# Laying the RWKV-7 chunk pairs on the partition halves by head parity in a one-core hybrid encoder layer

## The reference

```
def step(state, inp):
    r_t, w_t, k_t, v_t, kk_t, a_t = inp
    sa = jnp.einsum('bhvk,bhk->bhv', state, -kk_t)
    state = (state * w_t[:, :, None, :] + sa[..., None] * (kk_t * a_t)[:, :, None, :]
             + v_t[..., None] * k_t[:, :, None, :])
    return state, jnp.einsum('bhvk,bhk->bhv', state, r_t)
```

## Time and profile before

| | |
|---|---|
| median of 3 runs | 1093.29 us (1093.26 to 1096.49) |
| the profiled execution's own time | 1094.79 us |
| its span in the trace | 1092.7 us |
| TensorE busy | 1055.2 us, 97% of the span |
| VectorE, ScalarE, GpSimd busy | 608.6, 451.3, 30.9 us |
| chain that ended last | TensorE 80%, VectorE 9%, ScalarE 5% |

### The profile page before, as it was taken

One profiled execution on the slowest core, in us unless ns is written; L12 is line 12 of the kernel. 1 busy time (PEld: TensorE's weight loads), 2 busy tenths in 40 slices (PEclk: granted clock), 3 DMA queues, 4 the chain that ended last, 5 costly groups with the idle time before them and its releaser, 6 DMA issues.

```text
span 1092.7 us, 19121 instructions
## 1 busy us (share of the span) xinstructions
PE 1055.2 (97%) x8117; PEld 844.4 (77%) x8117; DVE 608.6 (56%) x858; ACT 451.3 (41%) x575; POOL 30.9 (3%) x50
## 2 busy tenths in 40 slices
PE   8999999999998999999999999999999999999997
PEld 5788667778876787787667778888888888878885
DVE  3499875356443469758656388663444533252446
ACT  5523643233323476755555464571222122222233
POOL 0100001000000000020000110000000000000000
PEclk9999999999999999999999999999999999999999
DMA  9977534211126331196311495304343423222201
GB/s 339 317 257 245 171 106 131 71 51 61 44 66 224 118 104 69 41 270 239 115 69 49 146 336 179 130 20 153 117 154 116 142 90 109 85 90 104 93 23 77
DMA packets 106780, 145.29 MB, mean 133 GB/s; under 512 B 3252, under 2 KB 86440, under 8 KB 106696
## 3 DMA queue, kind: packets, MB, share of 16 engines
q1 hardware_dynamic: 93544, 109.25, 30.2%
q0 software_dynamic: 5664, 21.19, 5.7%
q10 hardware_dynamic: 7488, 13.63, 3.3%
HBM read 128.33 MB, written 15.73 MB: 132 GB/s over the span
## 4 chain that ended last, share of the span: by engine, by line
PE 80%; DVE 9%; ACT 5%; DMA 2%; issue 2%; SPq 1%; ACTq 0%; POOL 0%; DVEq 0%
PE bank L2211 78%; DVE wlo L1466 2%; DVE Z L1466 1%; DVE q_lev L1466 1%; DMA qk<-early_out 1%; DMA raw<-in_w_in 1%; ACT whi L942 1%; SPq L814 1%; DVE near L1955 1%; ACT gate_row L957 1%; DVE mg L1466 1%; DVE ada_acc L1469 0%; DVE qk L1466 0%; PE bank L2792 0%; PE bank L2499 0%
## 5 line engine op out<-in xcount | busy, mean ns | idle before, releaser
L2211 PE MATMUL bank<-hhi,whi 128*128 128x512 f32 (+1 forms) x800 | 320.9, 401 | 4.3 <-ACT gate_row L957 2.6
L2211 PE MATMUL bank<-hhi,wlo 128*128 128x512 f32 (+1 forms) x800 | 310.0, 387 | 0.0
L2211 PE MATMUL bank<-hlo,whi 128*128 128x512 f32 (+1 forms) x800 | 309.7, 387 | 0.0
L1466 DVE TENSOR_TENSOR wlo<-raw,whi 128x2048 fp32r<-128x2048 f32 (+1 forms) x80 | 166.3, 2079 | 241.9 <-ACT whi L942 236.1
L942 ACT ACTIVATE whi<-raw 128x2048 fp32r<-128x2048 f32 (+1 forms) x76 | 135.5, 1783 | 227.6 <-PE bank L2211 178.1
L2211 PEld LDWEIGHTS bank<-hhi,whi 128*128 128x128 f32 x800 | 151.0, 189 | 46.4 <-issue 11.0
L2211 PEld LDWEIGHTS bank<-hhi,wlo 128*128 128x128 f32 x800 | 151.0, 189 | 31.5
L2211 PEld LDWEIGHTS bank<-hlo,whi 128*128 128x128 f32 x800 | 151.3, 189 | 28.6 <-issue 0.7
L2211 PE MATMUL bank<-whi,d_hi 128*128 128x512 f32 x160 | 62.3, 390 | 1.2 <-DVE hid L1466 1.2
L2211 PE MATMUL bank<-whi,d_lo 128*128 128x512 f32 x160 | 62.3, 389 | 0.0
L2211 PE MATMUL bank<-wlo,d_hi 128*128 128x512 f32 x160 | 62.2, 389 | 0.0
(11 more groups left out here) (369 smaller groups left out, 1503.6 us busy)
## 6 DMA issues: line engine op xcount, KB each, us to landing
raw<-in_w_in SPq DMA_DIRECT2D x33, 1024.0 KB, 5.5
raw<-in_f_in SPq DMA_DIRECT2D x22, 1024.0 KB, 4.9
raw<-in_ada_w SPq DMA_DIRECT2D x16, 1024.0 KB, 5.0
early_out<-gate_row ACTq DMA_DIRECT2D x52, 256.0 KB, 2.1
raw<-in_f_out SPq DMA_DIRECT2D x11, 1024.0 KB, 4.8
cond<-in_ada_w SPq DMA_DIRECT2D x8, 1024.0 KB, 10.7
sg<-early_out POOLq DMA_DIRECT2D x4, 1536.0 KB, 10.2
raw<-in_w_out SPq DMA_DIRECT2D x4, 1024.0 KB, 5.0
```

Of the source, the lines that this page charges most:

```text
L1466: return v.tensor_tensor(out_, a, b, op)
L2211: return t.matmul(out_, lhsT, rhs, start=start, stop=stop, skip_group_check=True)
```

## The change

The half of a matrix is chosen by the head parity `g`, not by the chunk `ab`. `UV` and `SC` become one tile for each pair. `rw r` needs one bank, not two. `take_r` is one ScalarE operation on 128 partitions where there were two on 64; `take_u` is two with a wait between them where there was one. `values_by_token` is 16 matmuls with 64 x 64 blocks of the identity where there were 4 transposes. The `BK` products are four operations on 64 partitions x 2048 elements where they were four on 128 x 1024. Two `ada_out` are moved ahead of `early(("rw fin", 4))` on VectorE. The two filling parts ahead of the last level of the first inverse are split: one stays, one moves between `values_by_token(1)` and `level_p(0, 4)`.

```
-    + ... [(("rw lev", 4), 2)]
+    + ... [(("rw lev", 4), 1), (("rw lev", 5), 1)]
...
-                for ab in range(2):
-                    nc.gpsimd.memset(UV[c % 2][ab][HALF[1 - ab], :], 0.0).then_inc(s_rw_zero, 1)
+                for g in range(2):
+                    nc.gpsimd.memset(UV[c % 2][HALF[1 - g], :, :, g, :], 0.0).then_inc(s_rw_zero, 1)
...
             def take_r(c, ab):
-                new = HALF[1 - ab]
-                for g in range(2):
-                    act.wait_ge(*full("rw r", c, ab, g))
-                    ps = bank_of("rw r", c, ab, g)
-                    do(rhs_u[new, g, :], ps[new, 0:256], ACT.Copy, scale=-1.0).then_inc(free_sem("rw r", c, ab, g), 1)
+                act.wait_ge(*full("rw r", c, ab))
+                do(rhs_u[:, :], bank_of("rw r", c, ab)[:, 0:256], ACT.Copy, scale=-1.0).then_inc(free_sem("rw r", c, ab), 1)
...
             def take_u(c, ab):
-                do(UV[c % 2][ab][new, :], bank_of("rw u", c, ab)[new, :], ACT.Copy).then_inc(free_sem("rw u", c, ab), 1)
+                new = bank_of("rw u", c, ab)[:, 0:256].rearrange("p (h t) -> p h t", h=4)
+                do(UV[c % 2][HALF[1], ab, :, 0, :], new[HALF[1]], ACT.Copy).then_inc(s_rw_values, 1)
+                act.wait_ge(s_rw_values, up(s_rw_values))
+                do(UV[c % 2][HALF[0], ab, :, 1, :], new[HALF[0]], ACT.Copy).then_inc(free_sem("rw u", c, ab), 1)
...
             for src, place in ((K, 0), (B, 1)):
-                for ab in range(2):
-                    tt(keys[:, :, ab, place ^ ab, :], pairs(src)[:, :, ab, :], pairs(cum)[:, :, ab, :], ALU.mult)\
-                        .then_inc(s_dve_step, 1)
+                for g, rows in enumerate(HALF):
+                    tt(keys[rows, :, place ^ g, :], chunks(src)[rows], chunks(cum)[rows], ALU.mult).then_inc(s_dve_step, 1)
                     dve.wait_ge(s_dve_step, up(s_dve_step))
...
             early(("rw fin", 3))
-            early(("rw fin", 4))
             for k in range(2):
                 ada_out(ADA[18 + k])
+            early(("rw fin", 4))
...
             def values_by_token(n):
                 ps = begin("rw v", n)
-                for hl in range(4):
-                    last = t.transpose(ps[:, hl * P:hl * P + P], V[:, hl, n * P:n * P + P], ident)
+                for ab in range(2):
+                    for hl in range(4):
+                        for g, rows in enumerate(HALF):
+                            last = mm(ps[rows, 256 * ab + 64 * hl:256 * ab + 64 * hl + 64],
+                                      V[rows, hl, n * P + 64 * ab:n * P + 64 * ab + 64], ident[rows, rows])
...
             def read_values(c, ab):
-                ps = [begin("rw r", c, ab, g) for g in range(2)]
-                pe.wait_ge(s_rw_zero, 2 * c + ab + 1)
-                for g in range(2):
-                    for hl in range(4):
-                        mm(ps[g][new, 64 * hl:64 * hl + 64], sc[:, 4 * g + hl, 0:64], uv[:, head_cols(hl, g)], hl == 0, False)
+                ps = begin("rw r", c, ab)
+                pe.wait_ge(s_rw_zero, 2 * c + 2)
+                for hl in range(4):
+                    for g in range(2):
+                        mm(ps[HALF[1 - g], 64 * hl:64 * hl + 64], SC[c % 2][:, g, 4 * ab + hl, 0:64], UV[c % 2][:, ab, hl, g, :],
+                           hl == 0, False)
...
             def new_values(c, ab):
-                for g in range(2):
-                    for hl in range(4):
-                        last = mm(ps[new, head_cols(hl, g)], XT[c % 2][new, 4 * g + hl, :], rhs_u[new, g, 64 * hl:64 * hl + 64])
+                for hl in range(4):
+                    for g in range(2):
+                        rows, cols_ = HALF[1 - g], slice(64 * hl, 64 * hl + 64)
+                        last = mm(ps[rows, cols_], XT[c % 2][rows, 4 * ab + hl, :], rhs_u[rows, cols_])
...
-            def last_levels(n, fourth, fifth):
+            def last_levels(n, fourth, between, fifth):
                 early(fourth)
                 level_t(n, 4)
                 if n + 1 < PAIRS:
                     values_by_token(n + 1)
+                early(between)
                 level_p(n, 4)
                 early(fifth)
                 level_t(n, 5)
```

More of the change, by code:

```diff
@@ L68 @@
     + [("rw kn mid", 2), (("rw sums", 0, 0), 2)] + [(("rw sums", n, x_), 4) for n, x_ in ((0, 1), (1, 0), (1, 1), (2, 0))]
-    + [("rw pro", 4)] + [((what, i), 1) for i in range(1, 4) for what in ("rw first", "rw lev")] + [(("rw lev", 4), 2)]
+    + [("rw pro", 4)] + [((what, i), 1) for i in range(1, 4) for what in ("rw first", "rw lev")] + [(("rw lev", 4), 1), (("rw lev", 5), 1)]
     + [(("rw loop", c, k), 1) for c in range(PAIRS - 1) for k in range(LOOP_PLACES)]
@@ L286, in bank_plan @@
         if last:
-            two("rw r", c, 0)
+            b.add("rw r", c, 0)
             b.add("rw u", c, 0)
             b.add("rw m", c, 0)
-            two("rw r", c, 1)
+            b.add("rw r", c, 1)
             b.add("rw u", c, 1)
@@ L485, in build @@
         XT = [at("XT0", 20, [P, 8, 64]), at("XT1", 22, [P, 8, 64])]
-        UV = [[at(f"UV{p}{ab}", 24 + 4 * p + 2 * ab, [P, T]) for ab in range(2)] for p in range(2)]
-        SC = [[at(f"SC{p}{ab}", 40 + 8 * p + 4 * ab, [P, 8, P]) for ab in range(2)] for p in range(2)]
+        UV = [at(f"UV{p}", 24 + 4 * p, [P, 2, 4, 2, 64]) for p in range(2)]
+        SC = [at(f"SC{p}", 40 + 8 * p, [P, 2, 8, P]) for p in range(2)]
         KBtok = [at(f"KBtok{ab}", 88.25 + 2 * ab, [P, T]) for ab in range(2)]
-        rhs_u = at("rhs_u", 92.25, [P, 2, 256])
+        rhs_u = at("rhs_u", 92.25, [P, 256])
         M = at("M", 94.25, [P, 4, 64])
@@ L1796, in begin_inverse @@
                 for q, rows in enumerate(QUARTER):
-                    own = slice(32 * (q % 2), 32 * (q % 2) + 32)
-                    v.copy_predicated(XB[rows, :, :], lmask(0, rows), SC[n % 2][1 - q // 2][rows, :, own])\
-                        .then_inc(s_rw_first, 1)
+                    own, g = slice(32 * (q % 2), 32 * (q % 2) + 32), 1 - q // 2
+                    v.copy_predicated(XB[rows, :, :], lmask(0, rows), SC[n % 2][rows, g, :, own]).then_inc(s_rw_first, 1)
                     dve.wait_ge(s_rw_first, up(s_rw_first))
@@ L2463, in level_t @@
                 ps = begin("rw t", n, i)
-                for head in range(8):
-                    cols_ = slice(32 * head, 32 * head + 32)
+                for item in range(8):
+                    cols_ = slice(32 * item, 32 * item + 32)
                     if i < RW_LEVELS - 1:
                         for q, rows in enumerate(QUARTER):
-                            own = slice(32 * (q % 2), 32 * (q % 2) + 32)
-                            last = mm(ps[rows, cols_], SC[n % 2][1 - q // 2][rows, head, own], X[rows, head, :])
+                            own, g = slice(32 * (q % 2), 32 * (q % 2) + 32), 1 - q // 2
+                            last = mm(ps[rows, cols_], SC[n % 2][rows, g, item, own], X[rows, item, :])
                         continue
@@ L2472, in level_t @@
                         upper, lower = QUARTER[2 * half], QUARTER[2 * half + 1]
-                        last = mm(ps[lower, cols_], SC[n % 2][1 - half][upper, head, 32:64], X[upper, head, :])
+                        last = mm(ps[lower, cols_], SC[n % 2][upper, 1 - half, item, 32:64], X[upper, item, :])
                 end(last, "rw t", n, i)
@@ L2511, in read_values @@
                 pe.wait_ge(*freed("rw v", c))
-                ps = [begin("rw r", c, ab, g) for g in range(2)]
-                pe.wait_ge(s_rw_zero, 2 * c + ab + 1)
-                for g in range(2):
-                    for hl in range(4):
-                        mm(ps[g][new, 64 * hl:64 * hl + 64], sc[:, 4 * g + hl, 0:64], uv[:, head_cols(hl, g)], hl == 0, False)
+                ps = begin("rw r", c, ab)
[4 more added lines that the diff above has]
+                           hl == 0, False)
             def read_state(c, ab):
-                new = HALF[1 - ab]
-                ps = [bank_of("rw r", c, ab, g) for g in range(2)]
+                ps = bank_of("rw r", c, ab)
                 pe.wait_ge(s_rw_state, 2 * c + ab + 1)
@@ L2524, in read_state @@
                     for g in range(2):
-                        last = mm(ps[g][new, 64 * hl:64 * hl + 64], AR[HALF[g], hl, 2 * c + ab, 0, :], M[HALF[g], hl, :], False, True)
-                        if hl == 3:
-                            end(last, "rw r", c, ab, g)
+                        last = mm(ps[HALF[1 - g], 64 * hl:64 * hl + 64], AR[HALF[g], hl, 2 * c + ab, 0, :], M[HALF[g], hl, :],
+                                  False, True)
+                end(last, "rw r", c, ab)
             def out_cols(hl, ab):
@@ L2544, in out_chunk @@
                     for g in range(2):
-                        last = mm(ps[HALF[g], out_cols(hl, ab)], UV[c % 2][ab][:, head_cols(hl, g)],
-                                  SC[c % 2][ab][:, 4 * g + hl, 64:128], False, True)
```

(13 more changed lines are left out.)

23 lines of the change are left out of this document (9 added, 14 removed).

## The result

The changed kernel takes 1085.57 us (median of 6 runs, 1084.09 to 1086.09) where the kernel before, on the same chip, takes 1093.28. The ratio is 0.992, with a 95% interval of 0.9905 to 0.9934: 7.2 to 10.4 us less, clear of the 0.3% that a measurement can miss. Two later groups of runs, each against the kernel before on its own chip, gave 0.9906 (0.9891 to 0.9920) and 0.9929 (0.9915 to 0.9943). The forecast was 1084.0. The span of the profiled execution went from 1092.7 to 1082.2 us.

The account below looks back on a forecast made before the run. TensorE, busy 97% of the span, was taken to bound the kernel. Terms -8.1 + 2.0 - 4.8 - 2.9 + 1.9 + 1.5 + 0.6 + 0.5 = -9.3 us gave 1084.0 us, range 1079.5 to 1089.5.

Parts of the forecast that it names:

- Alternation: `read_values` and `new_values`: products alternating between array halves save 0.51 and 0.50 us, eight times, 8.1 us less.
- Rival B: Alternation does not pay: issue or bank paces `read_values` and `new_values`, 8.1 shrinks to about 2; 1090 us, chance 0.10.
- Values: `values_by_token`: 16 products in place of 4 transposes take 1.08 us, not 0.58; four calls, 2.0 us more.
- Late conditioning: End of the last pair: TensorE's 3.3 us hole and its 1.5 us half-pace stretch go, 4.8 us less.
- Level four: First inverse: filling cuts the 1.86 us hole by 1.4 and removes 1.5 of half pace, 2.9 us less.
- BK products: VectorE ahead of the first inverse: longer products delay TensorE 1.9 us, plus one slow stretch of 1.5 us.
- `take_u`: ScalarE: two operations take 0.79 us, not 0.59; 0.2 us shows in pairs 0 to 2, 0.6 us more.
- Supply: Loop over pairs: more instructions in less time could make short holes grow, 0.5 us more, bounds 0 and 3.4.
- Rival C: Holes move instead of going: level four still starves and one loop level starves once; about 1088 us, chance 0.16.
- `issue` holes total over 3 us: Sign that the forecast is wrong: TensorE's holes without a releaser exceed 3 us in the profile after.
- Rival D: Slower: instruction supply bounds bursts around levels three and four, 3.4 us per starvation, slower from three on; chance 0.04.

Follow-up runs that it names:

- the kernel without alternation: The changed kernel with the loop over g outermost in `read_values` and `new_values`, four products in a row on one half: 1087.62 us, ratio 0.9947.
- the layout alone: The changed kernel with the two `ada_out` and the filling part back in their old places: 1091.79 us, ratio 0.9979 against the kernel before.

## Why the prediction was right

By its own steps, with the profiled executions before and after:

1. *Alternation.* -8.1 forecast. From start to start `read_values` went from 1.07 to 0.62 us and `new_values` from 1.07 to 0.61, 0.45 each where 0.51 and 0.50 stood; `read_state` with `out_state`, taken at 0, gave 0.17. Eight times: -8.6. Two row tiles write one bank in the new `new_values` at 0.68 us for 16, as fast as `read_values`, which uses all rows, at 0.69. The Trainium skill ("TensorEngine Tiling (Array Packing)", Restrictions and Gotchas) says that different row tiles cannot access the same PSUM bank at once; this trace shows no cost of it. Rival B falls, by this and by the kernel without alternation.
2. *Values.* +2.0 forecast, 1.07 against 0.58 us, four times: +2.0.
3. *Late conditioning.* -4.8 forecast; the wait and the slow stretch are gone, and alone or undone the edit weighs 4.0 us.
4. *Level four.* -2.9 forecast. This step failed as an edit: with the filling undone the new kernel is as fast. The hole that it was to cure came from a stretch of the stream that held only short matmuls, and the 28 more matmuls of each call in edit 2 put other instructions into that stretch. On the kernel before it gave 2.0.
5. *BK products.* +1.9 forecast for the wait: 2.28 - 0.45 = +1.8. The slow stretch of 1.5 that I added comes in some executions: not in the first profile of the changed kernel, in both later ones. Without it the forecast would have been 1082.5.
6. *`take_u`.* +0.6 forecast, three waits of 0.20: +0.6.
7. *Supply.* +0.5 forecast; this is the term that was mis-sized. The two holes of the loop before, 0.7 us in all, became four of 3.7 us: +3.0. Rival C, given 0.16, was half true: level four did not starve, but the loop did, and in the second profile level three of the first inverse lost 1.15 us. None of these holes drew a slow stretch, so the loop cost 3.0 and not 6. The prediction's own sign, "`issue` holes total over 3 us", came true: 3.7, 4.5 and 4.0 us in the three profiles.

For the profiled pair the terms sum to -8.6 + 2.0 - 4.8 - 3.4 + 1.8 + 0.6 + 3.0 = -9.4 us, with -3.4 for the hole and slow stretch of level four. The span fell by 10.5. The 1.1 us between is not assigned. Against the medians, -7.7 with an interval of -10.4 to -7.2, the forecast of -9.3 lies inside. That its sum meets the sum of the terms to 0.1 us is luck. Step 7 was 2.5 us too small; against it stood 1.5 us for a slow stretch that did not come in this execution, 0.5 us more from the matmuls and 0.5 us more from level four. Of the mechanisms, those of steps 1, 2, 3, 5 and 6 were right in the main; step 4 was right for the kernel before alone, and step 7 missed where the holes would go.

Rival D did not come: three starvations of 3.4 us each would have been needed, and the holes stayed at 1.3 us or less.

## What to carry to other kernels

Small matmuls in a row should go to different halves of the array, in output rows or in both, and the layout of the data decides whether they can. Once they do, count the instructions: in this kernel, where holes without a releaser stand at both ends of 254 instructions, those take 3.3 to 4.1 us, so a faster matmul in such a stretch gives part of its gain back. A long filling part inside the burst was worth 2.0 us where the whole stretch was short matmuls, and nothing that can be seen after the layout had moved the stretch: find the boundaries first. After an edit that lengthens an engine off the path, look at what that engine does between its last needed result and the signal: moving the signal ahead of an unrelated job was worth 3.1 us here, against 2.3 for the layout alone; the two cannot be told apart by their intervals, but the one is a single moved line.

## What was not expected of the hardware

Two holes without a releaser that follow each other at the next boundary end 127 matmuls and their weight loads apart, in every kernel that has such a pair. With the one or two semaphore instructions of TensorE that the packed trace has between them, that is 255 or 256 instructions. Holes further apart keep the step: in the kernel with the values issued twice, those that end at 244.79, 277.88 and 307.83 us lie 1792 and 1536 instructions apart, 7 and 6 times 256. The stretches with a hole at both ends take 3.84, 3.80, 4.07 and 3.85 us in the cases above, but 3.57 and 3.53 in the kernel with the filling undone, 3.57 in the second profile of the changed kernel and 3.29 in the kernel without alternation, so the pace is not one fixed number.

The trace's instruction queue moves one packet of 16 KB for each such stretch (64 in the kernel before, 65 in the changed one for 16458 matmuls and weight loads, 66 with the values issued twice), which fits a refill of the instruction stream. That the refill is the cause was argued from these counts and not shown by an experiment on the queue itself.

The same wait of 2.28 us at the same place was followed by a clock of 2.4 GHz in four profiled executions and of 1.2 GHz in four others. In the kernel before, the hole of 1.86 us was followed by 1.2 GHz; in the kernel with the values issued twice, the longer hole of 2.21 us in the loop was not (1.00 over 268 to 284 us).
